# The first token group's attention, taken out of its own stage and spread over the projection of groups 1 and 2

## What is computed

```
h = rmsnorm(x);  u = h @ w_in                       # 1024 -> 2560: xl, gl, q, k, v
lru_out = scan(a, b) * gelu(gl)                     # RG-LRU, 512 channels
for each head (4):                                  # causal, 64-wide halves of q and k
    w = softmax(q1 k1 / 8) - lam * softmax(q2 k2 / 8)
    o = rmsnorm(w @ v) * 0.8                        # 128 wide
x = x + rmsnorm([lru_out, o] @ w_out)
x = x + rmsnorm(swiglu(rmsnorm(x)))                 # 1024 -> 2816 -> 1024
x = x + rmsnorm(sigmoid(x @ ple_w_gate) * (p @ ple_w_proj))
```

## Time and profile before

| | us |
|---|---|
| median of 3 runs | 3056.19 |
| the profiled execution | 3059.22 |
| its span (first to last instruction) | 3057.5 |
| `project`, to TensorE's last matmul | 557.1 |
| `attend_first` with the gaps at both ends, to the first matmul of `feed` | 557.1 to 645.6 |
| TensorE busy | 2903.9 (95%) |
| VectorE busy | 1801.3 (59%) |
| ScalarE busy | 1357.2 (44%) |
| mean granted TensorE clock | 0.979 of full speed |

### The profile page before, as it was taken

One profiled execution on the slowest core, in us unless ns is written; L12 is line 12 of the kernel. 1 busy time (PEld: TensorE's weight loads), 2 busy tenths in 40 slices (PEclk: granted clock), 3 DMA queues, 4 the chain that ended last, 5 costly groups with the idle time before them and its releaser, 6 DMA issues.

```text
span 3057.5 us, 38197 instructions
## 1 busy us (share of the span) xinstructions
PE 2903.9 (95%) x14242; PEld 2371.0 (78%) x14242; DVE 1801.3 (59%) x2874; ACT 1357.2 (44%) x2491; POOL 233.5 (8%) x314
## 2 busy tenths in 40 slices
PE   7999999779999999999999999999999999999997
PEld 6778787557788887788888787788888778787865
DVE  6767767567356666665566666555656564343454
ACT  5655544534244445544444455444434453222233
POOL 0201011200000100001001100011011000000000
PEclk9999999779999999999999999999999999999998
DMA  5546343756654444543534335535332343232221
GB/s 181 182 140 228 130 147 118 229 181 197 201 145 121 123 119 138 168 128 100 136 117 110 103 126 179 138 94 138 107 102 74 118 165 111 83 93 87 76 83 49
DMA packets 377575, 402.57 MB, mean 132 GB/s; under 512 B 25641, under 2 KB 277845, under 8 KB 377392
## 3 DMA queue, kind: packets, MB, share of 16 engines
q1 hardware_dynamic: 360624, 341.32, 37.5%
q0 software_dynamic: 16768, 58.81, 5.4%
HBM read 341.19 MB, written 58.91 MB: 131 GB/s over the span
## 4 chain that ended last, share of the span: by engine, by line
PE 60%; DVE 11%; ACT 5%; issue 2%; POOL 0%; DMA 0%; SPq 0%; ACTq 0%; DVEq 0%; POOLq 0%
PE c_bank L2653 48%; PE b_S L2948 3%; PE b_O L2974 2%; DVE c_w L2331 2%; PE b_WT L2960 1%; PE b_S L2662 1%; PE b_O L2662 1%; ACT c_junk L2100 1%; DVE b_m L2538 1%; DVE c_rows L2342 1%; DVE c_rows L2349 1%; ACT b_p L2257 1%; DVE b_p L2531 1%; PE b_O L2976 1%; DVE c_hT L2369 1%
## 5 line engine op out<-in xcount | busy, mean ns | idle before, releaser
L2653 PE MATMUL c_bank<-c_hT,c_w 128*128 128x512 f32 (+1 forms) x4416 | 1027.0, 386 | 14.9 <-DVE c_hT L2369 14.9
L2653 PEld LDWEIGHTS c_bank<-c_hT,c_w 128*128 128x128 f32 x4416 | 797.3, 190 | 170.1 <-issue 18.5
L2653 PE MATMUL c_bank<-c_w,c_fT 128*128 128x512 f32 x2112 | 511.1, 395 | 0.5 <-DVE c_rows L2391 0.5
L2331 DVE TENSOR_TENSOR c_w<-c_raw,c_w 128x1024 fp32r<-128x1024 f32 x334 | 405.3, 1221 | 154.6 <-ACT c_w L2079 152.9
L2079 ACT ACTIVATE c_w<-c_raw 128x1024 fp32r<-128x1024 f32 x334 | 352.0, 1058 | 252.7 <-PE c_bank L2653 219.4
L2653 PEld LDWEIGHTS c_bank<-c_w,c_fT 128*128 128x128 f32 x2112 | 392.5, 189 | 88.1 <-issue 4.7
L2257 ACT ACTIVATE b_p<-b_S,b_nm 128x512 f32<-128x512 f32 (+3 forms) x288 | 180.3, 631 | 586.5 <-DVE b_nm L2539 586.5
L916 PE MATMUL a_bank<-a_w,a_hT 128*128 128x512 f32 x1152 | 284.2, 401 | 0.0
L2653 PE MATMUL c_bank<-c_w,c_hT 128*128 128x512 f32 x1152 | 275.9, 395 | 7.6 <-DVE c_w L2331 3.9
L2653 PEld LDWEIGHTS c_bank<-c_w,c_hT 128*128 128x128 f32 x1152 | 218.1, 191 | 54.7 <-DVE c_w L2331 4.3
L916 PEld LDWEIGHTS a_bank<-a_w,a_hT 128*128 128x128 f32 x1152 | 213.4, 188 | 51.9 <-issue 3.8
(11 more groups left out here) (377 smaller groups left out, 3316.5 us busy)
## 6 DMA issues: line engine op xcount, KB each, us to landing
c_raw<-in_ffn_w_gate SPq DMA_DIRECT2D x88, 512.0 KB, 4.9
c_raw<-in_ffn_w_up SPq DMA_DIRECT2D x88, 512.0 KB, 4.2
c_raw<-in_ffn_w_down SPq DMA_DIRECT2D x88, 512.0 KB, 3.9
a_raw<-in_w_in SPq DMA_DIRECT2D x40, 1024.0 KB, 5.2
b_k<-split_kT SPq DMA_DIRECT2D x72, 256.0 KB, 4.9
b_v<-split_v SPq DMA_DIRECT2D x36, 512.0 KB, 3.6
c_raw<-in_w_out SPq DMA_DIRECT2D x32, 512.0 KB, 5.6
c_raw<-in_ple_w_gate SPq DMA_DIRECT2D x32, 512.0 KB, 4.4
```

Source lines behind the costliest of these rows:

```text
L2331: V.tensor_tensor(w[:, e[1] % SLOTS, 1], raw[:, n % RAW], w[:, e[1] % SLOTS, 0].bitcast(F32), ALU.subtract).then_inc(split_ready, 1)
L2653: ins = T.matmul(out, lhs(k, a), rhs(k, b), start=first and k == 0 and n == 0, stop=end and k == blocks - 1 and n == 2)
```

## The change

The stage `attend_first` is gone, and `project` gets its work. A list `PLAN` has 77 places, 60 of them visits: S (scores of one or both halves), V (product with v of the step before), T (transpose of a head's result), W (transposes of the weights). For a step whose keys are 384 or 512 wide the scores are two visits, one PSUM bank each. Group 1 takes places 0 to 38 and group 2 the rest: one after each half job or `token_half`. In every engine's list the same place number (`place(i, c, x)`) calls `attend(k)`.

```diff
+    for s in range(HEADS * TILES):
+        h, t = divmod(s, TILES)
+        PLAN += [("S", s, (0,)), ("S", s, (1,))] if t >= 2 else [("S", s, (0, 1))]
+        PLAN += [("V", s - 1) if s else None, ("T", h - 1) if h and t == 1 else None, ("W", s)]
+    PLAN += [("V", HEADS * TILES - 1), None, None, None, ("T", HEADS - 1)]
+    PER_GROUP = 39
...
+    def visit_bank(k):
+        return banks[6 + VISITS.index(k) % 2]
```

TensorE's part, and the banks that the visits take. They are banks 6 and 7, which held the gates; the gates move to banks 0 and 1, where q and k are turned, so the turning now waits for the gates' tanh in all groups:

```diff
-            return (banks[7], banks[0]) if last else (banks[7], banks[6])
+            return (banks[7], banks[0]) if last else (banks[0], banks[1])
...
                 elif t >= 2:
                     pe.wait_ge(stage_lo, staged(i, Q, t - 2) + 1)
-                elif t == 1 and i == GROUPS - 1:
-                    pe.wait_ge(gate_free, 2 * LC * GROUPS)
-                elif t == 0 and i == GROUPS - 1:
+                elif t == 1 or i < GROUPS - 1:
+                    pe.wait_ge(gate_free, 2 * LC * (i + 1))
+                else:
                     pe.wait_ge(s_copied, 2)
...
+            def attend(k):
+                kind, n = PLAN[k][:2]
+                h, t = divmod(n, TILES)
+                cols = (t + 1) * P
+                v, bank = VISITS.index(k), visit_bank(k)
+                if v >= 2:
+                    freed(VISITS[v - 2])
+                if kind == "S":
+                    pe.wait_ge(q_in, 32 * (n + 1))
...
+                if kind == "W":
+                    pe.wait_ge(p_ready, n + 1)
...
+                if kind == "V":
+                    pe.wait_ge(wt_lo, n + 1)
...
-                        feature_job(i, 2 * c + f, slice(0, GROUP)).then_inc(job_done, 1)
+                        feature_job(i, 2 * c + f, slice(0, GROUP), 0)
+                        attend(place(i, c, 2 * f))
+                        feature_job(i, 2 * c + f, slice(0, GROUP), 1).then_inc(job_done, 1)
...
+                        attend(place(i, c, 2 * f + 1))
```

The loads of the first group's q, k and v move from SP to POOL. The first ones wait until all split stores of group 0 have landed:

```diff
+                if i == 1:
+                    for n in range(STAGES):
+                        pool.wait_ge(stage_out[n], 16 * 12 // STAGES)
+                    load_k(0)
+                    load_q(0)
+                    load_v(0)
```

The weight ring of `project` has 3 slots instead of 4, and the split of a group's second chunk moves from the end of the group before to its start. On ScalarE and VectorE the LRU's steps of c = 2 to 4 stand between the jobs instead of after them:

```diff
-    SLOTS = 4
+    SLOTS = 3
...
+                if i:
+                    split_in(CH * i + 1)
...
+                            if c == 3 and f == 0:
+                                root(i, 0)
+                            if c >= 2 and f == 0:
+                                gates(i, c - 2)
```

The four first loads and splits for `feed` move into the last group's v phase. The last group's stores of k and v move from POOL to SP, and the end of the stage no longer waits for stores to land or for POOL to drain (`no_gpsimd_drain=True`); `feed` waits for them where it reuses their memory:

```diff
+            sp.wait_ge(gate_free, 2 * LC * GROUPS)
+            sp.wait_ge(lru_out, 16 * LC * GROUPS)
+            for n in range(3):
+                load_first(n)
+            for t in range(TILES):
+                store_stage(K, t)
+                if t == 0:
+                    store_row(K, TILES)
+                store_row(V, t)
+                store_stage(V, t)
+                if t == 2:
+                    load_first(3)
+            store_row(V, TILES)
```

In `feed` the cached pages of the first three sequences are loaded at the first three items, after the page table, and the four first multiplications move; three small sums and a memset go to a later item:

```diff
-    MULT_S = [0, 1, 2, 3, 11, 13, 15, 17]
+    MULT_S = [2, 3, 4, 6, 11, 13, 15, 17]
...
+            for out, count in stores_out:
+                sp.wait_ge(out, count)
+            sp.dma_start(table[:], io["page_table"].rearrange("(o b) n -> o (b n)", o=1)).then_inc(table_in, 16)
...
+                if n < 3:
+                    load_pages(n)
```

More of the change, by code:

```diff
@@ L233, in project @@
         rows_ready = sem("a_rows_ready")
-        rows_out = [sem(f"a_rows_out{n}") for n in range(ROWS)]
         qk_turned = sem("a_qk_transposed")
@@ L615, in _ @@
                         copy_sample()
+                    if c == 4:
+                        attend(place(i, 4, 0))
+                        root(i, 1)
+                        gates(i, 2)
+                        attend(place(i, 4, 1))
+                        attend(place(i, 4, 2))
+                        attend(place(i, 4, 3))
                     if c in (5, 7):
@@ L637, in _ @@
                         split_in(CH * (i + 1))
-                    if t == 3 and not last:
-                        split_in(CH * (i + 1) + 1)
                     raw_rows(i, V, t)
@@ L890, in _ @@
                         rotate(i, K, TILES)
-                    if t == 3 and not last:
-                        split_lo(CH * (i + 1) + 1)
                     if t and last:
@@ L897, in _ @@
                         sample_lru(0)
+                    if t and last:
+                        split_second(t - 1)
+                    attend(place(i, 8, 2 * t + 1))
                     if t and not last:
@@ L1424, in feed @@
-def feed(nc, io, split, sems, pool_turn, shared, early, cached, first_stored):
+    return ([row_landed(n) for first in (LATE_ROW, len(USES)) for n in range(first - ROWS, first) if STORED[n]] +
+            [stage_landed(n) for first in (LATE_STAGE, 12 * GROUPS) for n in range(first - STAGES, first)], (small_out, 16 * (LC + 5)))
+def feed(nc, io, split, sems, pool_turn, shared, early, cached, landed):
     ctx = ExitStack()
@@ L1429, in feed @@
     ident, ident_r, mask, nlam, sub_gain = shared
-    w, raw, mixA, raw_in, split_hi, split_ready = early
-    pages, qb, table, table_in, pages_in, qb_in, free = cached
+    w, raw, mixA, raw_in, split_hi, split_ready, mix_at = early
+    pages, qb, table, table_in, pages_in, qb_in, held = cached
+    first_stored, stores_out, small_row_out = landed
     CH, SLOTS, RAW, AHEAD = 84, 4, 3, 2
@@ L2589, in _ @@
                 if n == SOFT - 1:
+                    for out, count in stores_out:
+                        dve.wait_ge(out, count)
+                    V.memset(wz[:], 0.0)
+                    V.reduce_sum(pair[:], ident[0:R, 0:R].rearrange("p (r c) -> p r c", c=2), axis=AX)
+                    V.reduce_sum(head[:], ident[:].rearrange("p (b h) -> p h b", h=HEADS), axis=AX)
+                    link(V.reduce_sum(fold[:], ident[:].rearrange("p (j r) -> p r j", r=RH), axis=AX))
                     dve.wait_ge(small_in, 16 * 4)
@@ L3002, in build @@
[L3002 to L3008 removed]
+            mix_at = base + 60960
@@ L3012, in build @@
-            held = 173792
+            rows_out, stage_out = ([sems.enter_context(nc.semaphore(f"a_{name}_out{n}")) for n in range(count)] for name, count in (("rows", 4), ("stage", 3)))
+            late_rows, late_stage = ([sems.enter_context(nc.semaphore(f"a_late_{name}_out{n}")) for n in range(count)] for name, count in (("rows", 4), ("stage", 3)))
+            lru_out, small_out = (sems.enter_context(nc.semaphore(f"a_{name}_out")) for name in ("lru", "small"))
+            stored = sems.enter_context(nc.semaphore("e_stored"))
```

760 lines of the change are left out of this document (353 added, 407 removed).

## The result

The changed kernel takes 3149.95 us (median of 4 runs, 3149.41 to 3155.64). The kernel before takes 3056.19; a fourth execution of it in the same comparison took 5931.75 us, and neither this median nor the ratio counts it. The ratio is 1.031, 95% interval 1.0298 to 1.0323: 3.1% slower, where 3045, a faster kernel, had been forecast. The profiled execution has a span of 3147.9 us, 90.4 more than before.

The account below looks back on a forecast made before the run. TensorE, busy 95% of the span, was taken as the bound. The terms -88.5 + 9.5 + 31 + 8.8 + 15 + 7 + 6 gave -11.2 us, from 3059.2 to 3048.0, or 3045 as median; range over all cases 3014 to 3070.

Parts of the forecast that it names:

- Part 1: Removed attention stage with its gaps, from 557.1 to 645.6: 88.5 us go.
- Part 2: The one block boundary left before feed: a gap of 9.5 us, bounds 6 and 18.
- Part 3: TensorE's attention work comes back inside the projection at full clock: 31 us, bounds 28 and 48.8.
- Part 4: First score visit: TensorE stands 6.8 us for the loads of k and q, bounds 4 and 12.
- Part 6: q's first transposes wait for each group's last tanh: 11 us plus 4 for the clock, bounds 4 and 24.
- Part 5: Lower TensorE clock after a stall: one above some 2 us costs up to 2 us more.
- Part 7: Other coupling with VectorE and ScalarE, served in order but not full: 7 us for both groups, bounds 1 and 25.
- Part 8: Start of feed: page loads and VectorE's page products make weight chunks late, net +6 us, bounds -3 and +14.
- The rule weighed: Skill page's drain of about 1.38 us per ScalarE table switch, 30 us over 22 extra switches; left out of the sum.
- The second: Rival: visits wait in order for VectorE and ScalarE; slower, 3080 at 1.2 us a visit, chance 0.17.
- point of decision: Second rival's threshold: it decides from 0.8 us a visit over 60 visits, against TensorE's gain of 48 us.
- Its sign: Second rival's evidence: groups 1 and 2 of the projection at 160 us each, with stalls on e_p or e_wT.

Follow-up runs that it names:

- e2: Changed kernel with only TensorE's visits and POOL's loads of q, k, v; no attention on VectorE or ScalarE, no POOL product; 3058.34 us.
- e1: Changed kernel with all attention visits and their q, k, v loads left out of the projection, zeros stored as the four heads; 3024.6 us.
- e3: Changed kernel with the block that begins a recurrence tile behind the third place of its chunk in VectorE's list instead of the first; 3118.91 us, ratio 1.0203.
- e5: Changed kernel with each tile's weights turned one tile later, the weighted sum in a buffer of its own; 3129.13 us, ratio 1.0236.
- e7: Changed kernel with VectorE's first four products of cached pages moved from items 2, 3, 4, 6 of feed to 9 to 12; 3148.27 us.
- e11: Changed kernel with page products at items 9 to 12 and the first page loads at items 5 to 7 instead of 0 to 2; 3140.62 us.
- e14: Changed kernel with turns, recurrence block and pages later, gates before q's last raw row, output sum at its visit; 3085.11 us, ratio 1.0085.

## Why the prediction was wrong, step by step

- **Part 1**, -88.5: as forecast.
- **Part 2**, the gap, 9.5 forecast, 6.7 measured. The sample row was stored 2.2 us behind TensorE's last work (1.4 forecast), the issues behind it took 2.5 us where 4.3 had been dated, and the boundary itself 1.7 instead of 3.2 (700.59 to 702.26).
- **Part 3**, TensorE's own work, 31 forecast, 31.0 measured (e2 against e1), with the estimated 2 us of lower clock in it.
- **Part 4**, the first visit, 6.8 forecast, 5.76 measured, with the DMA of q as its releaser. TensorE went on 0.8 us before the forecast time, if the 2.9 us that group 0 is late are added.
- **Part 6**, q's transposes, 11 forecast in three stalls of 2.6, 5.4 and 3.0; measured 2.50, 5.11 and 2.91. This part, called the dearest, came out as forecast; it was not the dearest. TensorE's timeline in the changed kernel, for parts 4 and 6:

```profile
103.24 0.63 PE L1212 MATMUL a_bank<-ident,a_rows 128*128 128x128 f32 x4 [2.50 <-ACT a_ri L612]
...
166.25 0.69 PE L1314 MATMUL a_bank<-e_k,e_q 128*128 128x128 f32 x2 [5.76 <-DMA e_q<-split_qT]
...
280.47 0.87 PE L1212 MATMUL a_bank<-ident,a_rows 128*128 128x128 f32 x3 [5.11 <-ACT a_ri L612]
...
477.45 0.68 PE L1212 MATMUL a_bank<-ident,a_rows 128*128 128x128 f32 x4 [2.91 <-ACT a_ri L612]
```

- **Part 5**, the clock: the mechanism was right, and the price fits on average (26 us over eighteen stalls, 1.4 each), but "up to 2 us" was too low a bound: behind the stall of 9.24 us the clock was still 0.50 from 437 to 440, and the twelve products there took 5.22 us (435.20 to 440.42) instead of 2.82. What failed more is the number of stalls it applied to: 6 us in the sum, 26.0 measured in groups 1 and 2 (busy time of the changed kernel less that of e2), since there were eighteen stalls and not four.
- **Part 7 is the step that failed.** It put 7 us for both groups, with 25 as its bound; the stalls on p, the outputs, the transposed weights, the scores bank and the stage buffer are 64 us. It reasoned with busy shares ("each group goes from 91 to 114 of about 145 us", "Neither is full") and then priced only the start of a group. The busy time was right, 115 us a group, and VectorE was indeed busy only 59%. What counts is another sum: what stands in the list between a visit's scores and its W. Worked out from the rows of the changed kernel, the chain itself is short: for 512 keys maximum and its scaling 0.83, two exponentials with their sums 1.6, coefficients 0.33, POOL's product 0.7, sum 0.75, some 4 us. Three places of 12 products are 8.5 us, which would be enough; but in chunks 2 to 4 a block of up to 8.8 us (3.6 waiting, 5.2 working) stands in between, and the two together are 13. Six of the eighteen stalls, 36.8 us, stand behind such blocks; the other twelve were not followed up one by one. All of that was to be read before: the order is in the code, and the reciprocal of 3.35 us in the trace. e3 and e5 show it from two sides.
- **Part 8**, the start of `feed`, 6 forecast with a bound of 14, 17.7 measured. VectorE's page products were priced; that the page loads keep the DMA engines busy (0.99) while `w_out` is loaded was not. The products were worth 4.4 us (e7), the loads 5.6 (e11), and 7.7 are left, part of them the price of the later pages.
- **Not in the sum at all:** 15.8 us over the rest of `feed`. Its rate was taken as unchanged, without a reason.
- **The rivals.** The second is what happened: visits wait in order for VectorE and ScalarE. It gave 3080 at 1.2 us a visit and had a chance of 0.17. Measured: 64 us of waits and 26 of clock over 60 visits, 1.5 us a visit, beyond its point of decision (0.8). With parts 4, 6 and 8 and the feed rate on top comes 3150. The sentence that spoke for it (splits of 2.3 us "in front of whatever comes") named too small a block. Its sign, groups 1 and 2 at over 160 us with stalls on e_p and e_wT, is there: 198 and 190 us.
- **The rule weighed.** 36 table loads stand in groups 1 and 2 of the changed kernel, 20 before: 16 more, where 22 had been counted. The next instruction follows the load of 1.28 us at once in 27 of the 36 cases (396.93, then 398.23), and in the other nine it comes 0.04 us behind VectorE's maximum or TensorE's product, for which it waits; the sum rightly went without a drain. The Trainium skill ("ScalarE: Activation LUTs", section "What ACT_TABLE_LOAD costs") is not borne out here on that point.

What stays open: the rate of c_hT with c_w in `feed`, below, and which of the stalls left in e14 (39 us) are of one kind. A shorter `lru_head` block was not tried.

## What to carry to other kernels

When short steps of one computation are woven into another's instruction lists, don't ask how busy the helping engine is, but add up, for each step, everything that stands before it in its engine's list, waits included, and compare this with the time between the two visits that it links. Place coarse blocks where nothing short is due behind them, or put the visits further apart; both work, and neither is complete, because the next step of the same list comes up. And give TensorE's stalls a second price for the clock behind them: here 26 us for 66.

## What the runs showed of the hardware

**A rate that differs between the two kernels, without a cause found.** 24 products with streamed c_w and standing c_hT, timeline of the kernel before and of the changed one, at the same place of the program:

```profile
2836.04 5.60 PE L2653 MATMUL c_bank<-c_hT,c_w 128*128 128x512 f32 x24
...
2843.34 5.63 PE L2653 MATMUL c_bank<-c_hT,c_w 128*128 128x512 f32 x24
```

```profile
2924.01 5.76 PE L2673 MATMUL c_bank<-c_hT,c_w 128*128 128x512 f32 x24
...
2931.46 5.77 PE L2673 MATMUL c_bank<-c_hT,c_w 128*128 128x512 f32 x24
```

The granted clock is 0.99 in both from 1970 to 2980 us, and products with mixA or fT have kept their rate (5.61 to 5.64). All twelve variants of the changed kernel have a median of 5.76 or 5.77, with and without visits, so it belongs to the layout or to `feed` itself. 32 bytes, 11 KB, the distance of the two buffers and c_w at 44 KB don't make it. c_w at 87 KB in the kernel before was not tried: that room is taken there. The page's group of these 4416 products has 1027.0 us before and 1044.1 after, and the one with c_w standing 275.9 and 282.1. That is 23 us together in all of `feed`; the 15.8 us are what is left of it, since TensorE stands less.

**POOL stands while VectorE runs on two inputs in the same memory.** A product on POOL that takes 0.5 us took 3.07, and ended when VectorE's split did. Timelines of POOL and VectorE in the changed kernel:

```profile
372.53 3.07 POOL L520 TENSOR_SCALAR e_p<-e_p,e_coef 128x256 f32<-128x256 f32 x1 [8.32 <-DVE e_coef L1037]
```

```profile
372.44 0.69 DVE L1045 TENSOR_TENSOR e_o<-e_o,e_oss 128x512 f32<-128x512 f32 x1
373.05 2.28 DVE L880 TENSOR_TENSOR a_w<-a_raw,a_w 128x2048 fp32r<-128x2048 f32 x1
375.63 0.48 DVE L1040 SCALAR_TENSOR_TENSOR e_p<-e_p,e_coef 128x256 f32<-128x256 f32 x1 [0.30 <-POOL e_p L520]
```

Both inputs of the first two VectorE instructions lie in SBUF. The kernel before has the same in `feed`: three products on POOL of 0.69 us each took 4.33 together, most of it while VectorE ran two splits (POOL at 2215.76, VectorE at 2215.47). Beside VectorE instructions with one input in PSUM (c_act, c_bank) two such products kept their 1.38 us together (changed kernel, 1144.75). It goes the other way too: VectorE's a_igx, which takes 0.69 us, took 1.40 beside a product of 0.70 us on POOL (changed kernel, 510.93). The Trainium skill says as much ("GPSIMD Engine Reference", section "1. Specifications": GpSimd shares its SBUF interfaces with VectorE, with contention when VectorE has two SBUF inputs), and this trace agrees. For a chain that goes through POOL between two steps of VectorE, a split in between cost its whole length here.

**The clock behind a stall.** Behind 8.5 us of idle time the granted clock is 0.50, the lower level (1.2 of 2.4 GHz), for three more us, and 0.73 in the next three. Behind 9.24 us it is still 0.50 from 437 to 440. In e2, with one stall of 5.5 us and no other of over 0.3 us, it is 0.96 over the first 90 us.
